# Matrix memory by token, modulation during the merge, waits per tile for barriers, in a kernel of three blocks

## What is computed

```python
# first block, matrix memory: 4 heads of 128; i_pre, f_pre are gates per head and token
qk = silu(causal_dwconv(concat([mq, mk]), m_conv_w, m_conv_b))     # 4 taps
num_t = sum_s dmat[t, s] * (q_t . k_s) * v_s                       # written in chunks in the reference
den_t = sum_s dmat[t, s] * (q_t . k_s)
h = num / maximum(abs(den), exp(-m_t))
hm = head_rmsnorm(h, m_norm_g)
ya = (sigmoid(mo) * hm) @ w_br_m
yb = differential_attention(...) @ w_br_d                          # 4 heads
mixed = sigmoid(g_a) * ya + sigmoid(g_b) * yb                      # the merge
x = x + mixed @ w_out
u = causal_dwconv(rmsnorm(x) @ w_up, ffn_conv_w, ffn_conv_b)       # 3 taps, 2 x 2816 columns
val, gt = split(u);  x = x + (gelu(gt) * val) @ w_down
x = x + sigmoid(rmsnorm(x) @ w_ple_gate) * (p @ w_ple)
# third block: shifts, scales and gates of three sublayers, from one vector c
mod = (silu(c) @ w_ada + b_ada)                                    # w_ada 1024 x 9216
```

## Time and profile before

| | |
|---|---|
| median of three runs | 2812.05 us |
| the profiled execution, its own time | 2812.49 us |
| its span (one core) | 2810.7 us |
| granted TensorE clock, mean over the span | 0.945 |
| busy: TensorE / weight load | 2515.1 us (89%) / 1998.7 us (71%) |
| busy: VectorE / ScalarE / GpSimd | 1377.8 us (49%) / 1018.1 us (36%) / 1034.5 us (37%) |
| transfers | 245.49 MB, mean 87 GB/s |

### The profile page before, as it was taken

How to read it: one execution, slowest core, us unless ns; L and a number is a source line. 1 busy time by engine, 2 the same in 40 slices (tenths; PEclk the granted TensorE clock), 3 DMA queues, 4 the chain that set the end, 5 groups by cost and what they waited for, 6 DMA issues and landing times.

```text
span 2810.7 us, 31316 instructions
## 1 busy us (share of the span) xinstructions
PE 2515.1 (89%) x11582; PEld 1998.7 (71%) x11582; DVE 1377.8 (49%) x1881; ACT 1018.1 (36%) x1294; POOL 1034.5 (37%) x758
## 2 busy tenths in 40 slices
PE   7968889879999789998898889999979998899996
PEld 5636668657777668776776677888858766588885
DVE  6373621478888865244444554232265343622225
ACT  4322422333334453466436533122234332322211
POOL 3202134435555344222343234445434203254442
PEclk9878999989999999999898999999989998899998
DMA  3102012324444322111122112222312101122221
GB/s 139 50 30 75 31 60 105 135 105 179 179 182 189 152 76 90 61 45 46 60 90 75 46 53 83 91 103 90 104 60 85 69 17 60 45 90 104 90 101 48
DMA packets 35811, 245.49 MB, mean 87 GB/s; under 512 B 3935, under 2 KB 3935, under 8 KB 7044
## 3 DMA queue, kind: packets, MB, share of 16 engines
q1 hardware_dynamic: 34704, 241.73, 23.8%
q10 hardware_dynamic: 1012, 2.45, 0.3%
HBM read 242.06 MB, written 2.11 MB: 87 GB/s over the span
## 4 chain that ended last, share of the span: by engine, by line
issue 57%; POOL 27%; PE 13%; DVE 2%; DVEq 0%; POOLq 0%; ACT 0%; ACTq 0%
POOL WL L279 27%; PE PS L314 4%; PE PS L315 4%; PE PS L316 4%; DVE X L2186 0%; DVE ARENA L2181 0%; DVE ARENA L1591 0%; DVE ARENA L1609 0%; POOLq L283 0%; DVEq L2185 0%; DVE ARENA L1616 0%; DVE ARENA L2313 0%; DVEq L1632 0%; PE PS L372 0%; POOLq L276 0%
## 5 line engine op out<-in xcount | busy, mean ns | idle before, releaser
L279 POOL TENSOR_TENSOR WL<-WT,WH 128x512 fp32r<-128x512 f32 x754 | 1034.3, 1403 | 1734.6 <-ACT WH L960 1225.9
L314 PE MATMUL PS<-HH,WH 128*128 128x512 f32 x1520 | 609.6, 401 | 47.4 <-DVE HL L1623 12.8
L316 PE MATMUL PS<-HH,WL 128*128 128x512 f32 x1520 | 599.9, 395 | 0.0
L315 PE MATMUL PS<-HL,WH 128*128 128x512 f32 x1520 | 599.6, 395 | 0.0
L314 PE MATMUL PS<-YH,WH 128*128 128x512 f32 x904 | 363.6, 402 | 59.2 <-ACT ARENA L954 18.9
L314 PEld LDWEIGHTS PS<-HH,WH 128*128 128x128 f32 x1520 | 290.5, 191 | 126.9 <-issue 26.5
L1238 ACT CAST WH<-WT 128x2048 fp32r<-128x2048 f32 x90 | 172.1, 1912 | 559.9 <-PE PS L314 559.9
L315 PE MATMUL PS<-YL,WH 128*128 128x512 f32 x904 | 358.3, 396 | 0.0
L316 PE MATMUL PS<-YH,WL 128*128 128x512 f32 x904 | 358.0, 396 | 0.0
L316 PEld LDWEIGHTS PS<-HH,WL 128*128 128x128 f32 x1520 | 290.0, 191 | 62.4
L315 PEld LDWEIGHTS PS<-HL,WH 128*128 128x128 f32 x1520 | 290.8, 191 | 58.0 <-issue 0.9
(11 more groups left out here) (285 smaller groups left out, 3387.2 us busy)
## 6 DMA issues: line engine op xcount, KB each, us to landing
WT<-weights SPq DMA_DIRECT2D x188, 1024.0 KB, 4.8
ARENA<-w_ada SPq DMA_DIRECT2D x36, 1024.0 KB, 6.7
X<-x_fm SPq DMA_DIRECT2D x4, 512.0 KB, 8.0
out_fm<-X SPq DMA_DIRECT2D x8, 256.0 KB, 2.0
ARENA<-rel_rows ACTq DMA_DIRECT2D x1, 1024.0 KB, 5.2
CON<-constants SPq DMA_DIRECT2D x1, 704.0 KB, 10.1
WT<-weights SPq DMA_DIRECT2D x1, 512.0 KB, 5.4
ARENA<-rows SPq DMA_DIRECT2D x1, 512.0 KB, 5.8
```

Source lines behind the costliest of these rows:

```text
L279: i = nc.gpsimd.tensor_tensor(WL[s][:, e], WT[s][:, e], WH[s][:, e].bitcast(F32), ALU.subtract)
L314: i0 = nc.tensor.matmul(o, w[0], r[0], start=first, stop=False, skip_group_check=True)
L315: nc.tensor.matmul(o, w[0], r[1], start=False, stop=False, skip_group_check=True)
L316: i2 = nc.tensor.matmul(o, w[1], r[0], start=False, stop=last, skip_group_check=True)
```

## The change

1. Matrix memory by token. The values get a column of ones per head (129 columns), and the product of a strip with them gives numerator and denominator in one, with tokens as partitions: ten matmuls per head of 128 rows by 129 columns (`m_values`). ScalarE copies them to NUM and adds the squares per token (`m_num`). Denominator, exp(-m), squares, root and factor are columns for all heads at once (MCOL, 128 x 16), computed once after the last head; 16 scalings, 16 transposes back (`mt_ready`), and one pass with gain and gate. TensorE's order is written out anew: scores of a head, one tile of the next head's panel or one value tile, values, another tile. ARG has two buffers. The value tiles come in halves (`vd_tile`) ahead of and between these. The transfer of the bias table BT is issued by ScalarE before the last head's values.
2. The five barriers go. The output products wait per block (`out_gemm`, `ready`), VectorE splits each block of the merge after the next ones are there (`mix_split`), into HH and HL; the first net starts from YH and YL. VectorE signals the end of the attention to SP (`da_done`).
3. The modulation moves: all 72 halves run during the merge and its output product. SP issues, from the third merge panel on, three pieces behind each panel; VectorE (`ada`) and ScalarE (`ada_sums`) take them in places written out by hand. silu(c) is held in two banks.
4. Feed-forward nets: four tiles in place of two of chunk 0 run on the unnormalised input (first net only, `raws=4`); the loop is one round shorter, and the last chunk's product is made during the down product of the chunk before (`early`); in three sums of squares the eighth block is added by a second matmul on TensorE in place of VectorE's addition (`two_parts`).
5. p is loaded after the modulation, the constants are waited for in `norm_sum`.

The diff, cut to its core and moved left by eight places:

```diff
-    stream(2, G_FFN1 + 2)
-    sp.wait_ge(sem("phase_end"), 3 * 3)
+    stream(2, G_MERGE + 2)
+    sp.wait_ge(sem("da_done"), 1)
     sp.dma_start(CROW, rows_in[:, 1536:1536 + D]).then_inc(sem("c_dma"), 16)
-    sp.dma_start(PIN, p_in).then_inc(sem("p_dma"), 16)
     for k in range(3):
         ada(k, k, first=True)
-    with sp.Fori(0, (CH - 1) // 2) as i:
-        for h in range(2):
-            g = G_FFN1 + 2 + 6 * i + 3 * h
-            for k in range(3):
-                panel(g + k, (G_FFN1 + 3 * h + k) % 2)
-            for k in range(3):
-                ada(3 + 6 * i + 3 * h + k, k)
-    panel(G_FFN1 + 3 * CH - 1, (G_FFN1 + 3 * CH - 1) % 2)
+    for i in range(12):
+        panel(G_MERGE + 2 + i, (G_MERGE + 2 + i) % 2)
+        for k in range(3 if i < 10 else 0):
+            ada(3 + 3 * i + k, k)
+    stream(G_MERGE + 14, G_FFN1)
     for k in range(3):
-        ada(NADA - 3 + k, k)
-    stream(G_PLE, n_panels)
+        ada(33 + k, k)
+    stream(G_FFN1, G_FFN1 + 2)
+    sp.wait_ge(sem("ada_used"), NADA)
+    sp.dma_start(PIN, p_in).then_inc(sem("p_dma"), 16)
+    stream(G_FFN1 + 2, n_panels)
...
+    def norm_sum(second=False, two_parts=False):
         n["sq"] += DT
-        n["acc"] += DT - 1
+        n["acc"] += DT - 2 if two_parts else DT - 1
+        pe.wait_ge(sem("con_dma"), 16)
         if second:
             pe.wait_ge(sem("sq_acc2"), DT - 1)
             nc.tensor.matmul(psb(2), ONES, ACC2, start=True, stop=True)
         pe.wait_ge(sem("sq_acc"), n["acc"])
-        nc.tensor.matmul(psb(3), ONES, ACC1, start=True, stop=True).then_inc(sem("ms_ready"), 1)
+        m = nc.tensor.matmul(psb(3), ONES, ACC1, start=True, stop=not two_parts, skip_group_check=True)
+        if two_parts:
+            pe.wait_ge(sem("sq_ready"), n["sq"])
+            m = nc.tensor.matmul(psb(3), ONES, SQ[:, 0, :], start=False, stop=True, skip_group_check=True)
+        m.then_inc(sem("ms_ready"), 1)
...
+    def m_max(h):
         if h:
...
         nc.tensor.matmul(psb(2), pick(h, 4), LROW[2][0:4, :], start=True, stop=True).then_inc(sem("mb_ready"), 1)
...
+    def m_score(h):
         pe.wait_ge(sem("mqk_ready"), 2 * (h + 1))
...
+        for i in range(NQ):
+            u = NQ * h + i
+            if u >= 2:
+                pe.wait_ge(sem("am_ready"), u - 1)
+            nc.tensor.matmul(PS[:, 3 + i % 2, 0:BLK[i]], KB[:, h % 2, P * i:P * (i + 1)], QB[:, h % 2, P * i:S],
...
+    def m_values(h):
+        if h:
+            pe.wait_ge(sem("num_ready"), h)
+        for t in range(NQ):
+            pe.wait_ge(sem("am_ready"), NQ * h + t + 1)
+            for e in range(t + 1):
+                o = OFF[e] + P * (t - e)
+                m = nc.tensor.matmul(PS[:, 5 + t // 2, M_V * (t % 2):M_V * (t % 2) + M_V], AMB[:, o:o + P], VM[:, e, h, :],
+                                     start=e == 0, stop=e == t, skip_group_check=True)
         m.then_inc(sem("nd_ready"), 1)
...
+    def vd_tile(q, half):
+        g = G_VD + q
+        if half == 0:
+            open_panel(g)
+        b = take()
+        for t in range(2):
+            tok = slice(P * (2 * half + t), P * (2 * half + t + 1))
+            for k in range(DT):
+                i0, i2 = exact3(PS[:, b, 256 * t:256 * t + 256], (HH[:, k, tok], HL[:, k, tok]), wtile(g % 2, 8, 256, k, 0, 256),
+                                k == 0, k == DT - 1)
+                if half == 0 and t == 0 and k == 0:
+                    used(g, i0)
+        i2.then_inc(sem("a_done"), 1)
...
+    for h in range(M_HEADS):
+        m_score(h)
+        if h + 1 < M_HEADS:
+            m_max(h + 1)
+            m_tile(h + 1, 1)
+        else:
+            vd_tile(0, 1)
+        m_values(h)
+        if h + 2 < M_HEADS:
+            m_tile(h + 2, 0)
+        elif h + 2 == M_HEADS:
+            vd_tile(0, 0)
+    vd_tile(1, 0)
+    for h in range(M_HEADS):
+        pe.wait_ge(sem("scaled_ready"), h + 1)
+        for t in range(NQ):
+            m = nc.tensor.transpose(PS[:, 4 + h, P * t:P * (t + 1)], NUM[:, h, t, 0:P], IDENT)
+        m.then_inc(sem("mt_ready"), 1)
+    vd_tile(1, 1)
...
+    ffn(G_FFN1, raws=4, src=(YH, YL))
...
+        if h + 1 < M_HEADS:
+            m_exp(h + 1)
+            m_silu(h + 1, 1)
+        else:
+            vd_copy(0, 1)
+            act.wait_ge(sem("rel_out"), 16)
+            act.dma_start(BT, bass.AP(rel_tmp.tensor, 1, [[1, P], [NREL, DA_HEADS], [1, S]])).then_inc(sem("bt_dma"), 16)
+        m_num(h)
+        if h + 2 < M_HEADS:
+            next_panel(G_MQK + h + 2)
+            m_silu(h + 2, 0)
+        elif h + 2 == M_HEADS:
+            next_panel(G_VD)
+            vd_copy(0, 0)
+    act.drain().then_inc(sem("msq_ready"), 1)
+    next_panel(G_VD + 1)
+    act.wait_ge(sem("mden_ready"), 1)
+    f(MCOL[:, 3, :], MCOL[:, 3, :], ACT.Sqrt, scale=1.0 / P).then_inc(sem("mrs_ready"), 1)
...
+    ada_at = [0]
+    def ada_sums(count):
+        for j in range(ada_at[0], ada_at[0] + count):
+            w = ADA[j // 2 % 3][:, D * (j % 2):D * (j % 2) + D]
+            act.wait_ge(sem("ada_mul"), j + 1)
+            i = f(w, w, ACT.Copy, accum_out=MOD[:, j:j + 1])
+            if j % 2:
+                i.then_inc(sem("ada_used"), 1)
+        ada_at[0] += count
     for jp in range(4):
         for q in range(2):
...
+            next_panel(G_MERGE + 3 * jp + q)
+            for e in range(2):
+                b = take()
+                i = f(GS[:, 2 * q + e, :], psb(b), ACT.Sigmoid)
+                free(i, b)
+                if q and e:
+                    act.drain().then_inc(sem("gs_ready"), 1)
+                if jp or q:
+                    ada_sums(3)
+            if jp == 0 and q == 0:
+                act.wait_ge(sem("c_dma"), 16)
+                f(CROWP, CROW, ACT.Silu).then_inc(sem("c_ready"), 1)
         next_panel(G_MERGE + 3 * jp + 2)
         skip(4)
+        if jp < 3:
+            ada_sums(6)
         act.wait_ge(sem("gs_used"), jp + 1)
-    end_phase()
-    out_gemm(G_OUT1, lambda k: par("norm_ffn", k))
+    for q in range(4):
+        next_panel(G_OUT1 + q)
+        skip(2)
+        if q:
+            for k in (2 * q - 2, 2 * q - 1):
+                raw(lambda k: par("norm_ffn", k), k, k + 1, YH)
+                ada_sums(2)
+    sqrt_ahead()
+    raw(lambda k: par("norm_ffn", k), 6, DT, YH)
+    settle()
...
         if conv:
+            high(g0 + 2, g0 % 2)
+            normalise(shift)
             mid(0)
-            sums(0, range(4))
+        else:
+            normalise(shift, last=t0 + 1, meanwhile=open_third)
...
-    def trail(k, gain=None):
+    def trail(k, gain=None, dst=(HH, HL)):
         if gain:
-            raw_lo(k, gain)
-        accumulate(k)
+            raw_lo(k, gain, dst)
+        if gain or k < DT - 1:
+            accumulate(k)
...
+    m_arg(0)
+    m_conv(1, 0)
...
+        m_weights(h)
...
+            m_arg(h + 1)
+            m_conv(h + 1, 1)
+        if h + 2 < M_HEADS:
+            m_conv(h + 2, 0)
...
+    dve.wait_ge(sem("msq_ready"), 1)
+    eg, msq, den, scl = (MCOL[:, c, :] for c in range(4))
+    nq = NUM[:, :, :, P:P + 1].rearrange("p h t n -> p (h t n)")
+    stt(out=den, in0=nq, scalar=-1.0, in1=nq, op0=ALU.mult, op1=ALU.max)
+    dve.drain()
+    tt(den, den, eg, ALU.max)
+    dve.drain()
+    ts(den, den, 1e18, None, ALU.min)
+    dve.drain()
+    tt(scl, den, den, ALU.mult)
+    dve.drain()
+    stt(out=scl, in0=scl, scalar=EPS * P, in1=msq, op0=ALU.mult, op1=ALU.add)
+    dve.drain().then_inc(sem("mden_ready"), 1)
+    dve.wait_ge(sem("mrs_ready"), 1)
+    nc.vector.reciprocal(scl, scl)
+    dve.drain()
+    for h in range(M_HEADS):
+        for t in range(NQ):
+            c = NQ * h + t
+            i = ts(NUM[:, h, t, 0:P], NUM[:, h, t, 0:P], scl[:, c:c + 1], None, ALU.mult)
+        i.then_inc(sem("scaled_ready"), 1)
+    for h in range(M_HEADS):
+        dve.wait_ge(sem("mt_ready"), h + 1)
+        stt(out=OG[:, h, :], in0=PS[:, 4 + h, :], scalar=par("m_norm", h), in1=OG[:, h, :], op0=ALU.mult, op1=ALU.mult)
+        dve.drain()
+        split(OG[:, h, :], h)
+    dve.drain()
...
+    dve.drain().then_inc(sem("da_done"), 1)
...
+    def ada(count):
+        for j in range(ada_at[0], ada_at[0] + count):
+            s, e = j // 2 % 3, j % 2
+            if e == 0:
+                dve.wait_ge(sem(f"ada_dma{s}"), 16 * (j // 6) + 16)
+            w = ADA[s][:, D * e:D * e + D]
+            tt(w, w, CROWP, ALU.mult).then_inc(sem("ada_mul"), 1)
+        ada_at[0] += count
+    def mix_split(k):
+        nc.vector.tensor_copy(HH[:, k, :], MIX[:, k, :])
+        dve.drain()
+        tt(HL[:, k, :], MIX[:, k, :], HH[:, k, :].bitcast(F32), ALU.subtract).then_inc(sem("mix_ready"), 1)
     for jp in range(4):
         skip(4)
+        if jp == 0:
+            dve.wait_ge(sem("c_ready"), 1)
+        ada(12 if jp else 6)
         dve.wait_ge(sem("gs_ready"), jp + 1)
         for j in range(2):
             dst = MIX[:, 2 * jp + j, :]
+            if jp == 3:
+                mix_split(3 * j)
             b = take()
```

(53 more changed lines are left out.)

370 lines of the change are left out of this document (145 added, 225 removed).

## The result

The changed kernel takes 2797.41 us (median of 5, 2797.18 to 2803.21) against 2812.72 us before (5 runs on the same chip): ratio 0.9945, 95% interval 0.9931 to 0.9958. It is 15 us faster, not 54. The profiled execution after took 2803.21 us, span 2801.4, so the two traces differ by 9.3 us, and what follows accounts for those.

What follows compares the result with a forecast made beforehand. TensorE was taken as busy nearly all the time in long products, losing time at the seams. Matrix memory 55, merge -51, first net 37 and the rest 13 sum to 54: 2812 - 54 = 2758 us, likely 2735 to 2790, outer range 2715 to 2798.

Steps and rivals of the forecast that it cites:

- stalls of this size cost 1 to 2 us each in clock afterwards ... I add 5: Matrix memory: TensorE's three 3.2 us stalls slow its clock afterwards; 5 us added, value tiles ending at 196.
- head period 20.4: Matrix memory: each head takes 20.4 us, with TensorE idle 3.2 us before the third score in three heads.
- The lower bound, 42: Matrix memory: lowest gain, if each stall leaves TensorE at 1.2 GHz for a whole tile; expected gain 55, upper bound 62.
- I take 7.8: Merge: a modulation piece and the panel behind it land in 7.8 us, giving 17.4 us per gate panel; loss 51.
- I take the smaller: Merge: 17.4 us per gate panel, not the 20.5 worked out for 1.2 GHz, which adds 31 us for ten panels.
- covered now by the late panel: Barrier after the merge, 10.3 us: splits per tile would leave under 1 us, but the late panel covers them.
- The net: First feed-forward net without modulation: gain 37, from output product 2, head 12, chunks 10, end 13; bounds 20 and 42.
- The rest, 12.8: Two barriers of 2.3 us, two last chunks of 3.05, three sums of squares skipping a 0.7 addition: gain 12.8, bounds 8 and 15.
- Rival (a): Merge: the queue does not hold, 11.4 us a panel, output starts at 140, not 200: 2698 us; chance 0.12.
- Rival (b): Matrix memory and merge: new waits leave TensorE at 1.2 GHz, 79 and 31 us more: 2868 us; chance 0.10.
- Rival (c): The walk holds, but matrix memory gives 42 or the merge loses 65: 2771 to 2785, inside the range; no separate chance.
- One sign of being wrong: Matrix memory: VectorE releasing most of TensorE's waits would mean its 12 us a head was mis-sized.

Runs made afterwards that it cites:

- e4: Changed kernel with, on VectorE in the matrix memory, the weighting of head h+1 ahead of the first convolution of head h+2: 2778.5 us, ratio 0.9887.
- e1: Changed kernel with each merge weight panel issued on SP one place earlier, ahead of the three modulation pieces it stood behind: 2727.5 us, ratio 0.9691.
- e3: Changed kernel with only the first three modulation pieces transferred, all 72 halves still multiplied and summed: 2726.3 us, ratio 0.9682.
- e12: Changed kernel with the merge's panels issued between the second and third modulation piece of a set: 2768.6 us, ratio 0.9845.
- e6: Changed kernel with ten extra matmuls of 512 columns ahead of each merge panel's first, to keep TensorE's clock up: 2797.7 us, ratio 0.9948.
- e7: Changed kernel with the first output product waiting until all eight merge blocks are split, not one by one: 2800.0 us, ratio 0.9953.
- e8: The kernel of e1 with the first output product waiting for all eight merge blocks: 2738.4 us, ratio 0.973.
- e11: Changed kernel with the last chunk's product made behind the previous chunk's down product again, in all three nets: 2810.1 us, ratio 0.9991.

## Why the prediction was wrong, by its own steps

The forecast was that the change gains 54 us; it gained 15 (9.3 between the traces). The mechanism of each part was right; the sizes failed, nearly all on the same side.

- **Matrix memory, "stalls of this size cost 1 to 2 us each in clock afterwards ... I add 5", "head period 20.4".** The stalls were there, near the size given (4.0, 3.2 and 3.3). Behind each the tile took 7.3 us at a clock of 0.74 to 0.77 where 5.5 was put, and the spread ahead of it was slow too. The periods were 24.4, 23.7 and 24.1 us, 10.6 over the walk. (The walk's own terms, 16.7 of work and 3.2 of wait, add up to 19.9, not 20.4.) By e4, whose warm head takes 18.3 us with 1.2 of waits, a head of this kernel is 17.1 of work, 3.9 of waits and 3.1 of clock: the work was right, and the clock had no term in the period. The first three tiles took 20.6 for 17.4, as the clock stood at 0.50 for the first 5.9 us of them, and started 2.7 us late. The stretch from the last scores to the transposes took 21.2 for 18.4, at full clock: TensorE waited 3.7 us for VectorE's scalings where 1.1 was put. So the value tiles ended at 211.3, not 196: the 5 us added for clock should have been some 13. The lower bound, 42, was built from just this (each stall leaves TensorE at 1.2 GHz for a whole tile), and 40.4 lies just outside it. In e4 8.8 us of waits taken away gave 14.5 us.
- **Merge, "I take 7.8" for a piece and the panel behind it.** The chain was right in its links (9.1 us of ScalarE's, then the transfer), shown by e1, e3 and e12. The transfer term is what was mis-sized: ScalarE stood 8.4 us for it at best and 9.3 in the mean, 14.9 us more in the ten periods than 7.8 each; the other terms came out 2.9 less. Ten periods came to 183.4 us where the prediction had 171.4: 12 of the 14 us missed here. The wait was longest, 10.2 to 10.7 us, behind the panels of branch products; the prediction gave these 16.1 us, and the first took 18.8. There six sums in a row release three pieces within 4.5 us: the third piece took 8.2 us and the panel behind it 10.2 from issue to landing at 373 us, and 5.9 and 8.0 behind a gate panel at 393. Of the rest, 3.2 us are at the start (the first held-back panel is cast 24.8 us after the attention, where 21.6 was put).
- **The clock in the merge, "I take the smaller".** That its slack covers the slow products held: they went from 11.0 to 12.5 to 14.0 us without lengthening the period, and e6 changed nothing. By the Trainium skill, TensorE: Matmul & The Clock Gate, section on HAM oscillation, a loop that waits for its data each time has a cold array each time; the merge agrees (0.87 where it was 0.97), but the 20.5 us a panel that the prediction worked out for this case didn't come, because the product's end isn't on the chain.
- **The barrier behind the merge, "covered now by the late panel".** Right: a wait for all eight blocks costs nothing with that cover (e7) and 5 to 11 us without it (e8).
- **The net.** The head gained 12 as forecast (79.6 us instead of 91.6 up to the same matmul), the chunks run at 32.85 us (295.6 us for nine) instead of 34.2, which is 12. The end gained 10, not 13, and TensorE now waits 2.0 us for a convolution at 927.0, since the last chunks stand outside the loop in another order. The 2 us of the output product did not come: it starts cold as before, behind the late panel (45.6 us).
- **The rest, 12.8.** Of it 3.6 is left in the trace, because an untouched stretch takes 6.8 us more there (below). Ahead of that stretch the gain had come to 7.3, behind it 3.1 followed, so the term was off by 2; e11 gives 13 us for the three last chunks alone, where the prediction had 11.5.
- **Rival (a)** was that the queue doesn't hold. It held as written; with the order of e1 the output product starts 146 us after the attention, near the 140 of that rival. **Rival (b)**, the clock, was the direction of part of the error, at a small share of its 110 us: some 13 in the matrix memory, of which 5 were in the forecast, and none in the merge. **Rival (c)** is what came, with both of its halves at once: 40.4 for its 42 in the matrix memory, and 65.1 for its 65 in the merge. By the prediction's own sum that is 2785; the net and the rest together missed some 14 us more.
- **The signs.** One sign of being wrong came true by its letter: VectorE releases most of TensorE's waits in the matrix memory. But the prediction's own three waits are VectorE's too, and its 12 us a head were right (12.6, 11.4 and 11.8), so the sign could not tell the cases apart.

What failed as a method: the terms with a bound were taken at the kind end (a transfer at its shortest, a stall at its wait alone), and five such choices add up; in the likeliest case's range, 2735 to 2790, there was no room for all of them at once. That 2797.4 still lies within the outer range, 2715 to 2798, is luck: its top was there for the lost clock of rival (b), not for what happened.

## What to carry to other kernels

A transfer that waits for a buffer to be used holds up everything behind it on its issuing queue, however idle the queue and the memory are: put the stream that sets the pace ahead of the one that has to wait, and check the slack in steps, not in bytes. Here one place was worth 71 us. (The Trainium skill, DMA: Bandwidth & Descriptors, section on one DMA's anatomy, has the reason: a semaphore is waited for on the issuing sequencer, before the transfer is dispatched. The trace agrees: SP stands 30 times for ScalarE's sums and issues the panel only behind the last piece, at 393.20.) When you price a short wait on TensorE, price the slow stretch around it with it: 8.8 us of waits taken away gave 14.5 us here, where they lay on the path, and the slow products of the merge cost nothing, where a transfer set the period.
